# Rotary embedding of an attention head moved from the iteration that uses it to the iteration that projects it, and the attention steps placed from slot 3 instead of slot 6.5

## The chip, the cores and the metric

The kernel runs on one core of a Trainium2 chip. The metric is device time in microseconds, the median of three runs. Five engines work from instruction queues of their own, each strictly in program order: PE (TensorE, matmuls), DVE (VectorE), ACT (ScalarE), POOL (GpSimd) and SP (issues the DMAs). An engine waits for another only where its next instruction carries a wait on a semaphore. A waiting instruction holds back everything behind it on that engine.

## The reference, cut to what matters

A layer with two groups of heads. 16 learned tokens are put ahead of 512 tokens of width 2048, the rows are normed, and one projection gives the columns of both groups. The change touches the second group, eight heads of differential attention. For each head (q and k 128 wide, two maps of 64; v 128 wide):

```
q = apply_rope(q, cos, sin);  k = apply_rope(k, cos, sin)     # x*cos + swap_halves(x)*sin
sc = q_c k_c^T / 8, causal mask, p_c = softmax(sc)            # c = 0, 1; queries in blocks of 128
o = (p_0 - lam * p_1) @ v
o = rms_norm(o, subln_w) * (1 - lambda_init) * silu(g)
```

The mixed heads go through an output projection (2048 by 2048), a norm and a residual add.

## The kernel before, in words

Sizes: D = 2048 features in KT = 16 slices of P = 128, SEQ = 512, META = 16, L = 528 tokens. Every projection is done in three matmuls on split weights (`w_hi`, `w_lo`) and split activations (`hn_hi`, `hn_lo`).

The work runs in 17 iterations i = 0 to 16 (`iterations`, lines 402 to 415). An iteration projects the four column tiles of one head pair or head (q = 0 to 3 in `tile_dve`: in an attention iteration these are `xk` = q, `xv` = k, `xr` = v, and the gate), and at the same time works on the head that the iteration before it projected. Iterations 8 to 15 project the attention heads, 9 to 16 attend (head n = i - 8). 10 to 15 are one loop body. 9 also finishes the other group (`gn` is true there and has placements of its own). 16 projects nothing: its PE stream is the first quarter of the output projection (`out_feature`).

The four tiles are 16 units of four weight slices each, 64 **slots** in an iteration. A slot is one feature slice: three matmuls of 512 columns, or six of 264 for k and v. The order on every engine is written out by generators. Each step of a head's work yields a place, a number in slots, and `upto` issues it when the stream comes to that place. On PE a step at place p stands behind slot p rounded up. DVE sorts its steps, the copies of the tiles among them, by their places (15.6, 31.6 and 47.6 for the copies, 63.6 for the gate). ACT and POOL issue one unit of weights at a time (`split_hi`, `split_lo` for unit k + 3) and behind it all steps with places up to 4k + 3. The split of k waits until PE is through unit k - 1 of this iteration (slot 4k - 1).

The steps of a query block qi = 0 to 3 lie at `attn_at(gn, qi)` plus an offset: +0 scores of both maps (PE, L752, or L749 and L750 for qi = 3), +1 and +2 mask, maximum and its negative (DVE, L1392 to L1394), +3 and +4 exponentials (ACT, L1027), +5 reciprocal and combination (DVE, L1398 to L1401), +7 transposes of the combined map (PE, L757, L759), +8 copy of these (ACT, L1032), +10 the product with v (PE, L765, L767), +11 its copy (DVE, L1405), +11.5 its squares (ACT, L1036). After qi = 3: +12.5 the variance (DVE, L1409), +12.7 the power -1/2 (POOL, L1101), +13 scaling (DVE, L1413), +14 transposes (PE, L773), +14.5 gate and store into the mixed rows (DVE, L1417).

The rotary embedding takes two parts. ACT swaps the halves of 64 (`swap_halves`, L880: four copies of 32 partitions) at places 16.3 (`xk` into `q_swap`) and 32.3 (`xv` into `k_swap`) of the projecting iteration, behind the tile's copy on DVE. DVE then makes seven instructions, L1372 to L1376 for q (into `qpad`) and L1379 to L1382 for k (into `kr`). Before the change these stand at places -0.5 to 0.2 of the next iteration.

Of the kernel before, what the change touches and what calls it, by code (L numbers as in the profile page):

```python
# [30 lines left out]
ALU = mybir.AluOpType  # L31
# [3 lines left out]
P = 128  # L35
D = 2048
SEQ = 512
META = 16
L = SEQ + META
KT = D // P  # L40
RW = 1024
NP_ = RW // P
HD = 64
# [74 lines left out]
def hybrid_layer(nc, x, meta_tokens, pre_norm_w, w_in, rwkv_mu, rwkv_w0, rwkv_w_up, rwkv_a0, rwkv_a_up,  # L118
# [3 lines left out]
    with ctx:  # L122
        def sb(name, shape, dt=F32):
            return ctx.enter_context(nc.sbuf_tensor(name, shape, dt))

        def sem(name):
            return ctx.enter_context(nc.semaphore(name))
# [21 lines left out]
        xk = sb("xk", [P, TP])  # L149
        xv = sb("xv", [P, TP])  # L150
# [86 lines left out]
        cos_t = carve("attn", "cos_t", L)  # L237
        sin_t = carve("attn", "sin_t", L)
        qpad = [carve("attn", f"qpad{m}", SEQ) for m in range(2)]
        kr = carve("attn", "kr", L)  # L240
        vt = carve("attn", "vt", TG * P)
        rt1 = carve("attn", "rt1", L)
        q_swap = carve("attn", "q_swap", SEQ)
        k_swap = carve("attn", "k_swap", L)
# [38 lines left out]
        def s(name):  # L283
            if name not in S:
                S[name] = sem(name)
            return S[name]
# [50 lines left out]
        def attn_stage_at(gn):  # L337
            return 12 if gn else 0

        def attn_at(gn, qi):  # L340
            return 20.5 + 12.2 * qi if gn else 6.5 + 13.0 * qi

        def mixed(i):

# [796 lines left out]
        def _(dve):  # L1141
            V = nc.vector
            steps = Steps(dve, "dve_step")
            TT, STT, TS = V.tensor_tensor, V.scalar_tensor_tensor, V.tensor_scalar
# [52 lines left out]
            def tile_dve(i, proj, work, gn):  # L1197
                for q in range(3):

                    yield 20 if q == 0 and gn and work == "attn" else 16 * q + 15.6  # L1200
                    o = tiles[(q + 1) % 2]
                    xt = (xk, xv, xr)[q]
                    if proj == "rwkv":
                        dve.wait_ge(s("x_based"), i * 3 + (q + 1))
                        STT(xt[:, PAD + 1:TP], o[:, EDGE:EDGE + L - 1], column(par, (8, 16, 0)[q], i),
                            xt[:, PAD + 1:TP], ALU.mult, ALU.add).then_inc(s("tile_freed"), 1)
                    else:
                        dve.wait_ge(s("unit_used"), i * 16 + (8 + 4 * q))
                        if work == "rwkv":
                            dve.wait_ge(s("bonus_taken" if q == 1 else "pads_made"), NP_)  # L1210
                            dve.wait_ge(s("vpad_made"), 2 * NP_)
                        else:
                            if q < 2:
                                dve.wait_ge(s("roped"), (i - NP_) * 2 + (q - 1))
                            else:
                                dve.wait_ge(s("vt_turned"), i - NP_)
                        full = FULL[proj][q]
                        n, at = (L, EDGE) if full else (SEQ, 0)
                        V.tensor_copy(xt[:, 0:n], o[:, at:at + n]).then_inc(s("tile_freed"), 1)
                yield 63.6  # L1220
                dve.wait_ge(s("gate_tanh"), i + 1)
                STT(gate[:], tanh_g[:], 1.0, tiles[0][:, 0:SEQ], ALU.add, ALU.mult).then_inc(s("tile_freed"), 1)
# [118 lines left out]
            def chain_dve(i, g, late, work, gn):  # L1341
                for c in range(GC):
# [10 lines left out]
                    dve.wait_ge(s("s_scaled"), m)  # L1353
                    STT(state, mb[:, 0:P], w_end[:, ch:ch + 1], state0, ALU.mult, ALU.add).then_inc(s("s_taken"), 1)  # L1354

            def attn_dve(i, gn):
                n = i - NP_
                at = attn_stage_at(gn)
                yield 9.3 if gn else at - 0.5
                if gn:  # L1360

                    dve.wait_ge(s("s_taken"), NP_ * NC)
                    dve.wait_ge(s("y_taken"), NP_ * NG)
                    V.memset(qpad[0][HD:P, :], 0.0)
                    V.memset(qpad[1][0:HD, :], 0.0).then_inc(s("arena_freed"), 1)
                yield 15 if gn else at - 0.3
                if gn:
                    dve.wait_ge(s("rope_in"), 32)
                if not gn:
                    dve.wait_ge(s("roped"), n * 2 - 2)  # L1370
                dve.wait_ge(s("tile_freed"), i * 4 - 1)
                steps.quiet(TT(rt1[:, 0:SEQ], xk[:, 0:SEQ], cos_t[:, META:L], ALU.mult))  # L1372
                dve.wait_ge(s("swapped"), n * 8 - 4)
                steps(TT(q_swap, q_swap, sin_t[:, META:L], ALU.mult))
                TT(qpad[0][0:HD, :], rt1[0:HD, 0:SEQ], q_swap[0:HD, :], ALU.add)
                TT(qpad[1][HD:P, :], rt1[HD:P, 0:SEQ], q_swap[HD:P, :], ALU.add).then_inc(s("roped"), 1)  # L1376
                yield 19.2 if gn else at + 0.2
                dve.wait_ge(s("roped"), n * 2 - 1)
                steps.quiet(TT(rt1, xv[:, 0:L], cos_t, ALU.mult))  # L1379
                dve.wait_ge(s("swapped"), n * 8)  # L1380
                steps(TT(k_swap, k_swap, sin_t, ALU.mult))
                TT(kr, rt1, k_swap, ALU.add).then_inc(s("roped"), 1)  # L1382
                for qi in range(4):
                    base = attn_at(gn, qi)
                    c = n * 4 + (qi - 3)
                    at = EDGE if qi == 3 else 0
                    width = META + (qi + 1) * P
                    for m, o in ((0, ma), (1, mb)):
                        yield base + 1 + m
                        dve.wait_ge(s("score_done"), c * 2 + (m - 1))  # L1390
                        d = o[:, at + width - P:at + width]
                        steps(TT(d, d, c32v("causal"), ALU.add))  # L1392
                        steps(V.reduce_max(at_max[:, m:m + 1], o[:, at:at + width], AX))
                        TS(at_neg[:, m:m + 1], at_max[:, m:m + 1], -HD ** -0.5, None,  # L1394
                           ALU.mult).then_inc(s("neg_made"), 1)
                    yield base + 5
                    dve.wait_ge(s("exp_made"), c * 2)
                    steps(V.reciprocal(at_inv, at_sum))  # L1398
                    steps(TT(at_inv[:, 1:2], at_inv[:, 1:2], lam[:], ALU.mult))
                    steps(TS(prob[1][:, 0:width], prob[1][:, 0:width], at_inv[:, 1:2], None, ALU.mult))  # L1400
                    STT(prob[0][:, 0:width], prob[0][:, 0:width], at_inv[:, 0:1], prob[1][:, 0:width], ALU.mult,  # L1401
                        ALU.subtract).then_inc(s("combined"), 1)
                    yield base + 11
                    dve.wait_ge(s("pv_done"), c)
                    V.tensor_copy(o_sb[:, qi * P:(qi + 1) * P], mb[:, 0:P]).then_inc(s("o_taken"), 1)  # L1405
                at = attn_at(gn, 3)
                yield at + 12.5
                dve.wait_ge(s("o_squared"), n * 4)
                TS(at_var, at_var, 1.0 / P, SUB_EPS, ALU.mult, ALU.add).then_inc(s("ovar_taken"), 1)  # L1409
                yield at + 13  # L1410
                dve.wait_ge(s("o_powed"), n)
                o3 = o_sb.rearrange("p (m d) -> p m d", m=4)
                TT(o3, o3, at_pow.unsqueeze(2).broadcast_to([P, 4, P]), ALU.mult).then_inc(s("o_scaled"), 1)  # L1413
                yield at + 14.5
                dve.wait_ge(s("o_turned"), n)
                dve.wait_ge(s("gate_moved"), i)
                STT(mixed(i - 1), gate2[:], gate_sub[:], ma[:, 0:SEQ], ALU.mult, ALU.mult).then_inc(s("o_made"), 1)  # L1417

            def split_y_dve():
                for k in range(KT):  # L1420
                    yield max(4 * k - 7, -1) + 0.1 if k < KT - 1 else 200
                    dve.wait_ge(s("y_hi"), k + 1)
                    TT(hn_lo[:, k, 0:SEQ], ymix[:, k, :], hn_hi[:, k, 0:SEQ].bitcast(F32),  # L1423
                       ALU.subtract).then_inc(s("y_lo"), 1)

            def body(i, proj, work, gn):
                gens = rwkv_work(i, work, gn, stage_dve, gn_dve, inv_dve, chain_dve)
                if work == "attn":
                    gens.append(attn_dve(i, gn))
                gens.append(tile_dve(i, proj, work, gn) if proj is not None else split_y_dve())  # L1430
                upto(begin(*gens), 1000)
                steps.clear()
# [42 lines left out]
```

## Time and profile before

| | us |
|---|---|
| median of three runs (lowest, highest) | 1552.87 (1552.44, 1555.18) |
| span of the profiled execution | 1549.4 |
| PE busy | 1436.7 |
| DVE busy | 767.5 |
| ACT busy | 576.3 |
| POOL busy | 476.7 |
| PE waiting for the rotary embedding (L752 for L1382), 890 to 1410 | 15.3 in 5 waits |

The profile shows one execution. Its own time is the span; the 3.5 us by which the median is longer lie around it (start and end of the program). The iterations with attention begin at about 892 us. The page's chain of the work that ended last is 76% PE. In the lists a row names the line of the code, the engine, the instruction, what it writes and what it reads; what stands in brackets at the end of a timeline row is the idle time before it and what ended it.

### The profile page before, as it was taken

How to read it: one execution, taken by the hardware profiler on the slowest of the kernel's cores; microseconds unless marked ns; L12 is line 12 of the kernel's file. 1: busy time of each engine (PE TensorE's matmuls, PEld its weight loads, DVE VectorE, ACT ScalarE, POOL GpSimd, SP SyncE). 2: the span in 40 equal slices, each digit the busy share in tenths (PEclk: the TensorE clock that was granted, in tenths of full speed). 3: DMA queues.
4: the chain of work that ended last, by engine and by line, in shares of the span. 5: the costliest groups of instructions: out<-in, count | busy, mean ns of one | idle time of the engine just before them, and what ended most of it. 6: DMA issues, size and time to landing. Idle time of an engine off the chain costs nothing.

```text
span 1549.4 us, 26552 instructions
## 1 busy us (share of the span) xinstructions
PE 1436.7 (93%) x9929; PEld 1257.3 (81%) x9929; DVE 767.5 (50%) x1560; ACT 576.3 (37%) x1204; POOL 476.7 (31%) x361
## 2 busy tenths in 40 slices
PE   5998999999999999999999988999999999989994
PEld 4988889788897888988879786978878879768883
DVE  2326566665666666667666544344343443540003
ACT  5332343333434334343333253434444434432321
POOL 2341232222322223232232232334333333324442
PEclk9999999999999999999999999999999999999997
DMA  5221111111111111111111121222222222215322
GB/s 190 71 84 42 42 44 49 50 41 41 42 47 44 43 44 42 47 42 41 47 42 49 50 73 50 70 69 70 69 68 68 61 68 68 68 58 205 117 95 111
DMA packets 151637, 101.43 MB, mean 65 GB/s; under 512 B 6446, under 2 KB 140688, under 8 KB 150416
## 3 DMA queue, kind: packets, MB, share of 16 engines
q1 hardware_dynamic: 151584, 100.71, 21.2%
q8 instruction: 35, 0.57, 0.1%
q14 instruction: 18, 0.15, 0.0%
HBM read 96.49 MB, written 4.19 MB: 65 GB/s over the span
## 4 chain that ended last, share of the span: by engine, by line
PE 76%; DVE 14%; issue 4%; ACT 3%; DMA 1%; POOL 1%; DVEq 0%; SPq 0%; ACTq 0%; POOLq 0%
PE tile L517 39%; PE ma L623 3%; PE tile L784 2%; PE tile L785 2%; PE tile L786 2%; PE ma L644 1%; PE ma L658 1%; DVE arena L1333 1%; PE ma L651 1%; PE mb L709 1%; PE ma L661 1%; DVE arena L1308 1%; PE mb L765 1%; PE ma L786 1%; PE ma L784 1%
## 5 line engine op out<-in xcount | busy, mean ns | idle before, releaser
L1086 POOL TENSOR_TENSOR w_lo<-w_raw,w_hi 128x512 fp32r<-128x512 f32 x324 | 429.3, 1326 | 1012.7 <-ACT w_hi L843 1012.6
L517 PE MATMUL tile<-hn_hi,w_hi 128*128 128x264 f32 (+1 forms) x1696 | 455.5, 331 | 0.0
L517 PE MATMUL tile<-hn_hi,w_lo 128*128 128x264 f32 (+1 forms) x1696 | 436.6, 320 | 0.0
L517 PE MATMUL tile<-hn_lo,w_hi 128*128 128x264 f32 (+1 forms) x1696 | 435.7, 320 | 0.0
L843 ACT CAST w_hi<-w_raw 128x512 fp32r<-128x512 f32 x324 | 200.3, 619 | 425.3 <-PE tile L517 315.1
L517 PEld LDWEIGHTS tile<-hn_hi,w_hi 128*128 128x128 f32 x1696 | 280.0, 190 | 25.6 <-issue 7.2
L517 PEld LDWEIGHTS tile<-hn_hi,w_lo 128*128 128x128 f32 x1696 | 277.6, 190 | 13.3
L517 PEld LDWEIGHTS tile<-hn_lo,w_hi 128*128 128x128 f32 x1696 | 277.3, 190 | 11.0 <-issue 0.5
L1321 DVE TENSOR_TENSOR arena<-ma,c 128x384 f16<-128x384 f32 x120 | 66.7, 556 | 54.7 <-PE ma L644 52.5
L979 ACT ACTIVATE arena<-ma 128x384 f16<-128x384 f32 x120 | 58.5, 487 | 89.0 <-PE ma L658 88.5
L1330 DVE CAST arena<-ma 128x384 f16<-128x384 f32 x120 | 66.6, 555 | 49.3 <-PE ma L661 47.9
L623 PE MATMUL ma<-arena 128*128 128x192 f32 x288 | 59.6, 343 | 12.2 <-issue 12.2
L1405 DVE COPY arena<-mb 128x128 f32<-128x128 f32 x32 | 9.3, 290 | 103.6 <-PE mb L767 103.6
L976 ACT ACTIVATE arena<-ma 128x384 f32<-128x384 f32 x72 | 35.2, 489 | 68.2 <-PE ma L651 68.2
L623 PEld LDWEIGHTS ma<-arena 128*128 128x128 f32 x288 | 47.8, 195 | 15.3 <-issue 13.9
L784 PE MATMUL tile<-w_hi,hn_hi 128*128 128x512 f32 x128 | 53.6, 419 | 5.5 <-DVE hn_lo L1423 5.5
L1308 DVE TENSOR_TENSOR arena<-arena,c 128x384 f16<-128x384 f16 x144 | 52.2, 404 | 0.8
L785 PE MATMUL tile<-w_lo,hn_hi 128*128 128x512 f32 x128 | 51.6, 403 | 0.0
L786 PE MATMUL tile<-w_hi,hn_lo 128*128 128x512 f32 x128 | 51.3, 401 | 0.0
L1101 POOL TENSOR_TENSOR arena<-arena,power 128x4 f32<-128x4 f32 (+2 forms) x25 | 39.1, 1566 | 33.1 <-DVE arena L1409 13.3
L992 ACT ACTIVATE arena<-arena 128x128 f32<-128x128 f32 x72 | 28.8, 400 | 52.7 <-DVE arena L1354 36.5
L658 PE MATMUL ma<-arena 128*128 128x128 f16 x360 | 41.3, 223 | 3.8 <-DVE arena L1321 3.8
(252 smaller groups left out, 2242.5 us busy)
## 6 DMA issues: line engine op xcount, KB each, us to landing
w_raw<-w_in SPq DMA_DIRECT2D x260, 256.0 KB, 2.8
w_raw<-w_out SPq DMA_DIRECT2D x64, 256.0 KB, 2.5
big<-x SPq DMA_DIRECT2D x4, 1024.0 KB, 8.9
arena<-x SPq DMA_DIRECT2D x4, 1024.0 KB, 9.7
out<-big SPq DMA_DIRECT2D x4, 768.0 KB, 3.6
arena<-post_norm_w SPq DMA_DIRECT2D x1, 1024.0 KB, 4.9
out<-big SPq DMA_DIRECT2D x4, 256.0 KB, 2.5
arena<-table_rope SPq DMA_DIRECT2D x2, 264.0 KB, 2.9
```

Of the source, the lines that this page charges most:

```text
L517: last = mm(o[:, at:at + n], w[:, slot, cols], t[:, kt, tok:tok + n], start=(kt == 0 and w is w_hi and t is hn_hi), stop=(kt == KT - 1 and ...
L623: last = mm(ma[:, c * 256:c * 256 + P + CH], pad[:, cs[c], :], apad_r[:, cs[c], :], start=True, stop=True)
L658: last = mm(bank(0, c), bl(xt16, c), bl(z16, c), start=True, stop=True)
L784: mm(banks[t], hn_hi[:, k, y], w_hi[:, k % RING, :], start=(k == 0), stop=False)
L785: mm(banks[t], hn_hi[:, k, y], w_lo[:, k % RING, :], start=False, stop=False)
L786: last = mm(banks[t], hn_lo[:, k, y], w_hi[:, k % RING, :], start=False, stop=(k == KT - 1))
L843: nc.scalar.copy(w_hi[:, slot, :], w_raw[:, slot, :]).then_inc(s("hi_done"), 1)
L979: A(x16, ma[:, 0:W], ACT.Copy).then_inc(s("x_taken"), 1)
L1086: T(w_lo[:, slot, :], w_raw[:, slot, :], w_hi[:, slot, :].bitcast(F32), ALU.subtract).then_inc(s("lo_done"), 1)
L1308: level = lambda l, o: TT(o, g3(ab_hi), level_masks[:, l, :].unsqueeze(1).broadcast_to([P, GC, P]), ALU.mult)
L1321: TT(g3(z16), g3(ma[:, 512:512 + W]), ident16.unsqueeze(1).broadcast_to([P, GC, P]), ALU.add).then_inc(s("zz_taken"), 1)
L1330: V.tensor_copy(xt16, ma[:, 512:512 + W]).then_inc(s("xt_taken"), 1)
```

## The change

- `attn_at` for the iterations without `gn` (10 to 16) gives 3.0 + 13.2 qi instead of 6.5 + 13.0 qi. The four blocks begin at 3, 16.2, 29.4 and 42.6 instead of 6.5, 19.5, 32.5 and 45.5. All steps of the head move with them, on all engines.
- The seven DVE instructions of the rotary embedding become `rope_q` and `rope_k`. A new generator `rope_next`, in every attention iteration that also projects (9 to 15), issues them for the head that is being projected: places 48.2 and 54.5 (62.5 and 64.0 in iteration 9). It first waits until all eight scores of the present head are done, since `qpad` and `kr` have one buffer. Iteration 9 still makes its own head's embedding at 15 and 19.2.
- `swap_halves`, the splits of the weights, the copies of the tiles and the POOL steps keep their code.

```diff
         def attn_at(gn, qi):
-            return 20.5 + 12.2 * qi if gn else 6.5 + 13.0 * qi
+            return 20.5 + 12.2 * qi if gn else 3.0 + 13.2 * qi
...
-            def attn_dve(i, gn):
-                n = i - NP_
-                at = attn_stage_at(gn)
-                yield 9.3 if gn else at - 0.5
...
-                yield 15 if gn else at - 0.3
...
-                if not gn:
-                    dve.wait_ge(s("roped"), n * 2 - 2)
-                dve.wait_ge(s("tile_freed"), i * 4 - 1)
+            def rope_q(n):
+
+                dve.wait_ge(s("tile_freed"), (n + NP_ - 1) * 4 + 2)
                 steps.quiet(TT(rt1[:, 0:SEQ], xk[:, 0:SEQ], cos_t[:, META:L], ALU.mult))
                 dve.wait_ge(s("swapped"), n * 8 - 4)
                 steps(TT(q_swap, q_swap, sin_t[:, META:L], ALU.mult))
                 TT(qpad[0][0:HD, :], rt1[0:HD, 0:SEQ], q_swap[0:HD, :], ALU.add)
                 TT(qpad[1][HD:P, :], rt1[HD:P, 0:SEQ], q_swap[HD:P, :], ALU.add).then_inc(s("roped"), 1)
-                yield 19.2 if gn else at + 0.2
+
+            def rope_k(n):
                 dve.wait_ge(s("roped"), n * 2 - 1)
+                dve.wait_ge(s("tile_freed"), (n + NP_ - 1) * 4 + 3)
                 steps.quiet(TT(rt1, xv[:, 0:L], cos_t, ALU.mult))
                 dve.wait_ge(s("swapped"), n * 8)
                 steps(TT(k_swap, k_swap, sin_t, ALU.mult))
                 TT(kr, rt1, k_swap, ALU.add).then_inc(s("roped"), 1)
+
+            def rope_next(i, gn):
+
+                yield 62.5 if gn else 48.2
+                dve.wait_ge(s("score_done"), (i - NP_) * 8)
+                rope_q(i - (NP_ - 1))
+                yield 64.0 if gn else 54.5
+                rope_k(i - (NP_ - 1))
...
                 if work == "attn":
                     gens.append(attn_dve(i, gn))
+                    if proj is not None:
+                        gens.append(rope_next(i, gn))
```

The order on the engines moves at three places of the loop body (iterations 10 to 15). The first is DVE around the copy of the k tile (`COPY xv`), with the masks and maxima of the third query block (`ma` and `mb` are the scores of the two maps). Before:

```order
L1405 COPY arena<-mb 128x128
L1208 REGISTER_ALU
L1219 COPY xv<-tile 128x528
L1390 ISA
L1392 TENSOR_TENSOR ma<-ma,c 128x128
L1393 TENSOR_REDUCE arena<-ma 128x1
L1394 TENSOR_SCALAR arena<-arena 128x1
L1392 TENSOR_TENSOR mb<-mb,c 128x128
L1393 TENSOR_REDUCE arena<-mb 128x1
L1394 TENSOR_SCALAR arena<-arena 128x1
```

In the changed kernel, where these instructions have line numbers that are 13 higher:

```order
L1418 COPY arena<-mb 128x128
L1403 ISA
L1405 TENSOR_TENSOR ma<-ma,c 128x128
L1406 TENSOR_REDUCE arena<-ma 128x1
L1407 TENSOR_SCALAR arena<-arena 128x1
L1405 TENSOR_TENSOR mb<-mb,c 128x128
L1406 TENSOR_REDUCE arena<-mb 128x1
L1407 TENSOR_SCALAR arena<-arena 128x1
L1208 REGISTER_ALU
L1219 COPY xv<-tile 128x528
L1411 RECIPROCAL arena<-arena 128x2
```

The copy of the k tile stood ahead of the maxima and now stands behind them, ahead of the reciprocal.

The second is ACT in the same stretch: the swap of `xv` and the two exponentials of the third query block (the rows with 128x400).

```order
 L1036 ACTIVATE arena<-arena 128x128
 L842 REGISTER_ALU
 L843 CAST w_hi<-w_raw 128x512
 L880 ACTIVATE arena<-xv 32x528 x4
-L840 ISA
-L842 REGISTER_ALU
-L843 CAST w_hi<-w_raw 128x512
 L1026 ISA
 L1027 ACTIVATE arena<-ma,arena 128x400
 L1027 ACTIVATE arena<-mb,arena 128x400
+L840 ISA
 L842 REGISTER_ALU
```

One split of weights moves from between swap and exponentials to behind them; the swap stays ahead of the exponentials.

The third is DVE at the end of the head. Before, from the copy of the last product with v on:

```order
L1405 COPY arena<-mb 128x128
L1409 TENSOR_SCALAR arena<-arena 128x4
L1413 TENSOR_TENSOR arena<-arena 128x512
L1417 ISA
L1417 SCALAR_TENSOR_TENSOR big<-gate,gate_sub,ma 128x512
```

In the changed kernel:

```order
L1362 TENSOR_TENSOR arena<-arena 64x512
L1363 TENSOR_TENSOR arena<-arena 64x512
L1418 COPY arena<-mb 128x128
L1366 ISA
L1367 REGISTER_ALU
L1368 TENSOR_TENSOR arena<-xv,arena 128x528
L1370 TENSOR_TENSOR arena<-arena 128x528
L1371 TENSOR_TENSOR arena<-arena 128x528
L1422 TENSOR_SCALAR arena<-arena 128x4
L1426 TENSOR_TENSOR arena<-arena 128x512
L1430 ISA
L1430 SCALAR_TENSOR_TENSOR big<-gate,gate_sub,ma 128x512
```

The q part of the embedding (L1359 to L1363) now ends right ahead of the copy, and the k part (L1368 to L1371) stands between the copy and the variance.

## Rows read from the trace of the kernel before

**Rows 1.** The page's first line: the span.

```profile
span 1549.4 us, 26552 instructions
```

**Rows 2.** Waits of PE, 890 to 1410: total us, times, longest.

```profile
PE ma L752 <- DVE arena L1382: 15.3, 5, 3.1
...
PE ma L757 <- DVE arena L1401: 6.1, 5, 2.0
...
PE ma L773 <- DVE arena L1413: 4.4, 2, 3.9
```

**Rows 3.** Waits of PE in the last iteration, 1325 to 1400.

```profile
PE tile L784 <- DVE hn_lo L1423: 5.5, 2, 3.2
...
PE ma L757 <- DVE arena L1401: 3.5, 3, 2.0
```

**Rows 4.** Timeline of DVE, rotary in iteration 12: start us, us.

```profile
1078.12 0.69 DVE L1372 TENSOR_TENSOR arena<-xk,arena 128x512 f32<-128x512 f32 x1
...
1084.34 1.65 DVE L1382 TENSOR_TENSOR arena<-arena 128x528 f32<-128x528 f32 x1
```

**Rows 5.** Timeline of PE, iteration 12: scores, transposes. Start, us, [idle before].

```profile
1086.04 0.51 PE L752 MATMUL ma<-arena 128*128 128x144 f32 x2 [3.05 <-DVE arena L1382]
...
1109.02 0.83 PE L752 MATMUL ma<-arena 128*128 128x400 f32 x2
...
1115.46 0.49 PE L757 MATMUL ma<-c,arena 128*128 128x128 f32 x3
```

**Rows 6.** Timeline of DVE, third query block of iteration 12.

```profile
1107.77 0.71 DVE L1219 COPY xv<-tile 128x528 f32<-128x528 f32 x1 [0.64 <-PE tile L517]
...
1111.83 0.15 DVE L1394 TENSOR_SCALAR arena<-arena 128x1 f32<-128x1 f32 x1
...
1113.83 0.17 DVE L1398 RECIPROCAL arena<-arena 128x2 f32<-128x2 f32 x1 [1.84 <-ACT arena L1027]
...
1114.69 0.64 DVE L1401 SCALAR_TENSOR_TENSOR arena<-arena 128x400 f32<-128x400 f32 x1
```

**Rows 7.** Timeline of ACT, same stretch: swap of xv, first exponential.

```profile
1108.51 2.64 ACT L880 ACTIVATE arena<-xv 32x528 f32<-32x528 f32 x4
...
1112.54 0.59 ACT L1027 ACTIVATE arena<-ma,arena 128x400 f32<-128x400 f32 x1
```

**Rows 8.** Timeline of POOL, iteration 16.

```profile
1365.61 1.38 POOL L1086 TENSOR_TENSOR w_lo<-w_raw,w_hi 128x512 fp32r<-128x512 f32 x1 [1.51 <-ACT w_hi L843]
```

**Rows 9.** Timeline of DVE, iteration 16, beside that POOL instruction.

```profile
1365.91 1.52 DVE L1401 SCALAR_TENSOR_TENSOR arena<-arena 128x400 f32<-128x400 f32 x1
```

**Rows 10.** Timeline of PE, end of the head of iteration 12.

```profile
1130.93 1.05 PE L765 MATMUL mb<-arena 128*128 128x128 f32 x8
...
1133.82 0.39 PE L517 MATMUL tile<-hn_hi,w_hi 128*128 128x512 f32 x1
...
1135.22 0.65 PE L773 MATMUL ma<-c,arena 128*128 128x128 f32 x4
```

**Rows 11.** Timeline of ACT, same stretch: a weight split.

```profile
1130.42 0.62 ACT L843 CAST w_hi<-w_raw 128x512 fp32r<-128x512 f32 x1 [0.66 <-PE tile L517]
```

**Rows 12.** Timeline of POOL, same stretch: that unit's low part, the power.

```profile
1131.12 1.26 POOL L1086 TENSOR_TENSOR w_lo<-w_raw,w_hi 128x512 fp32r<-128x512 f32 x1 [1.95 <-ACT w_hi L843]
...
1133.43 1.01 POOL L1101 TENSOR_TENSOR arena<-arena,power 128x4 f32<-128x4 f32 x1 [1.05 <-DVE arena L1409]
```

**Rows 13.** Timeline of DVE, end of iteration 9.

```profile
949.80 0.29 DVE L1405 COPY arena<-mb 128x128 f32<-128x128 f32 x1 [2.67 <-PE mb L767]
```

**Rows 14.** Windows of 8 us after long PE waits: busy; then clock, DMA, GB/s.

```profile
1023.40:1031.40 8.00, 7.96 (x32) 6.60 (x33) 2.42 (x10) 1.99 (x7) 1.28 (x1) 0.81 0.11 33
...
1086.00:1094.00 8.00, 7.96 (x44) 6.85 (x44) 3.11 (x11) 3.19 (x9) 2.00 (x2) 1.00 0.22 64
...
1208.30:1216.30 8.00, 7.99 (x24) 6.52 (x25) 2.42 (x10) 1.56 (x5) 0.98 (x1) 0.63 0.11 33
...
953.60:961.60 8.00, 7.95 (x30) 6.53 (x31) 5.36 (x8) 1.88 (x4) 1.08 (x1) 0.71 0.13 36
```

More of the change, by code:

```diff
@@ L1354, in chain_dve @@
                     STT(state, mb[:, 0:P], w_end[:, ch:ch + 1], state0, ALU.mult, ALU.add).then_inc(s("s_taken"), 1)
-            def attn_dve(i, gn):
-                n = i - NP_
-                at = attn_stage_at(gn)
-                yield 9.3 if gn else at - 0.5
[L1360 to L1365, printed above, removed]
-                yield 15 if gn else at - 0.3
-                if gn:
-                    dve.wait_ge(s("rope_in"), 32)
-                if not gn:
-                    dve.wait_ge(s("roped"), n * 2 - 2)
-                dve.wait_ge(s("tile_freed"), i * 4 - 1)
+            def rope_q(n):
+                dve.wait_ge(s("tile_freed"), (n + NP_ - 1) * 4 + 2)
                 steps.quiet(TT(rt1[:, 0:SEQ], xk[:, 0:SEQ], cos_t[:, META:L], ALU.mult))
@@ L1382, in attn_dve @@
                 TT(kr, rt1, k_swap, ALU.add).then_inc(s("roped"), 1)
+            def rope_next(i, gn):
[4 more added lines that the diff above has]
+                rope_k(i - (NP_ - 1))
+            def attn_dve(i, gn):
+                n = i - NP_
+                if gn:
+                    yield 9.3
+                    dve.wait_ge(s("s_taken"), NP_ * NC)
+                    dve.wait_ge(s("y_taken"), NP_ * NG)
+                    V.memset(qpad[0][HD:P, :], 0.0)
+                    V.memset(qpad[1][0:HD, :], 0.0).then_inc(s("arena_freed"), 1)
+                if gn:
+                    yield 15
+                    dve.wait_ge(s("rope_in"), 32)
+                    rope_q(i - NP_)
+                    yield 19.2
+                    rope_k(i - NP_)
                 for qi in range(4):
```

## The prediction, made before the changed kernel was run

> **What bounds the kernel now.** I read the page first, for its span of 1549.4 us [rows 1]. The median of the three runs is 3.5 us above it; I work out a change of the span and add it to the median. PE carries the chain that ended last, so what counts is where PE waits. In the list of PE's waits for the attention stretch the largest entry is the first scores of a head waiting for the last instruction of the rotary embedding, 15.3 us in 5 waits, the longest 3.1 [rows 2]. These are iterations 11 to 15. The other two entries are small and partly in iterations 9 and 16: transposes waiting for the combined map, and the last transposes waiting for the scaling. In a loop iteration PE waits for nothing else of size. Next come the timelines of one steady iteration, 12, engine by engine, to find how much room each chain has before its PE step. A slot takes 0.70 us (three matmuls of 512) or 0.73 (six of 264): two slots and the product with v take 2.89 and four slots with it 4.29 in rows 10, so a slot there is 0.70.
>
> **What goes.** The seven embedding instructions run from 1078.12 to 1085.99 and the scores start 0.05 later, after 3.05 us of idle PE [rows 4, 5]. Moved into the iteration before, they have ended about 15 slots before the scores need them. The scores at slot 3 then wait for the copy of v only, which ACT makes at the start of the iteration within two slots. So 15.3 us go. Iteration 10 has no such wait, and the first of the seven attending iterations has its own embedding as before, so there is nothing more to win here. After the five waits TensorE's granted clock is 1.00 over 8 us in two iterations (one shown), 0.81 and nearly that in two (one shown), 0.63 in one [rows 14]: in three of five cases the clock fell to its lower level (1.2 of 2.4 GHz) after the wait. That costs 8 x (0.19 + 0.19 + 0.37) = 6.0 us, 1.2 a wait. It goes as well, if nothing takes its place.
>
> **What comes: the swap ahead of the third block's exponentials.** Let S be the start of that block's scores on PE. In iteration 12 S is 1109.02 and the transposes start at S + 6.44, seven slots after the scores, without a wait [rows 5]. The second maximum is ready at 1111.83 + 0.15, S + 2.96 [rows 6]. Before the change ACT had finished the swap of `xv` by then: it began at 1108.51, right behind the copy of the tile at 1107.77, and took 2.64 us [rows 6, 7]. Now the scores stand behind slot 30 and the copy of the k tile belongs behind slot 31. DVE makes the copy behind both maxima: S + 3.0 to S + 3.7. The swap waits for it and stands ahead of the exponentials in ACT's queue: S + 3.7 to S + 6.4. From the first exponential to the reciprocal it is 1.29 us (1112.54 to 1113.83), from the reciprocal to the end of the combination 1.50 (1113.83 to 1114.69 + 0.64) [rows 6, 7]. That gives S + 9.2 against the 6.44 of PE's stream: a wait of at least 2.8 us in each of the six loop iterations.
>
> It is likely more. The next split on ACT (0.62 us, rows 11) is overdue and follows the exponentials at S + 7.7, and POOL makes its low part 0.7 later, as 1130.42 to 1131.12 shows [rows 11, 12]: from S + 8.4 to S + 9.7. The last instruction of the combination would start at S + 8.5. In iteration 16 the same instruction started 0.30 us behind such a POOL instruction and took 1.52 instead of 0.64 us, until after that one's end [rows 6, 8, 9]. The same here ends it at S + 10.3, a wait of 3.9. I take 3.9; the ends are 2.8 and 4.1. The Trainium skill says the same of the mechanism (SBUF — State Buffer, "Who interferes with whom"): a DVE instruction with two SBUF inputs contends with a GpSimd instruction that reads SBUF, and whoever issues first blocks the other. The trace agrees; by the rule the value is 3.9, and without it 2.8.
>
> **What comes: the end of the head.** Let V be the start of the last product with v, 1130.93 in iteration 12 [rows 10]. The last transposes were at V + 4.29, four slots on, just in time: the power on POOL began at 1133.43, 1.79 before them [rows 10, 12]. POOL makes it behind the low part of unit 17, for which ACT's split waits for the end of slot 55. Before, V lay behind slot 56, so that low part started at 1131.12, V + 0.2, which is 0.9 after slot 55's end (slot 56 of 0.70 lies between). Now V lies behind slot 53, slot 55 ends at V + 2.9, the low part runs from V + 3.8 to V + 5.1, the power cannot start earlier, and the transposes are at V + 6.9 instead of V + 4.29, a wait of 2.6 us. The place of the power, 55.3 instead of 58.2, falls into the same unit on POOL, so its order does not change; only PE arrives three slots earlier.
>
> DVE adds to it. The k part of the embedding, three instructions of 0.7 without a collision [rows 4], stands between the copy and the variance: copy at V + 1.6, variance at V + 4.0 instead of just ahead of the power, V + 2.3. That alone is inside the 5.1 of POOL. But its last instruction runs when the low part wants to start, which pushes that by some 0.3. If the q part, which runs beside two low parts, collides twice (1.0 each, as 1.65 against 0.69 in rows 4), the copy comes late, the k part collides too, and the wait is 3.9. I take 2.9; the ends are 2.6 and 3.9.
>
> **Iterations 9 and 16.** In 9 the seven instructions, 7 x 0.7 = 4.9 us, now stand ahead of the last product's copy, before which DVE was idle for 2.67 [rows 13]. The copy comes 2.2 later, and PE's wait for the scaling grows from 3.9 [rows 2] to 6.1: +2.2. In 16 the embedding leaves the start, where no PE wait hung on it. Its 3.5 us of waits for the combined map [rows 3] come from exponentials held behind a split, and at the new places they stand ahead of it: I take 2.5 less, the end being about even, since the late power costs PE there too while the last feature needs less of a wait. Bounds: 3.5 less to 2 more.
>
> **The clock.** A wait of 3.88 us in iteration 9 is followed by 8 us at 0.71 [rows 2, 14], 2.3 us lost. Six new waits of 3.9 at 2.3 and six of 2.9 at 1.2 make 21, less the 6.0 that go: +15. The ends: none of the twelve lowers the clock, -6, and all do at 3.0 (8 x 0.37), +30. This is the widest term.
>
> **The sum.** -15.3 + 6 x 3.9 + 6 x 2.9 + 2.2 - 2.5 = +25.2 us of waiting, +15 of clock: +40. The span comes to 1590 and the median to 1593. The cheaper ends of the waits (2.8, 2.6) with a clock term of 0 give 1552.9 + 16.8, about 1570. The dearer ones (4.0 and 3.4) with +25 give 1552.9 + 28.8 + 25, about 1607.
>
> **The rivals.**
> - Only the swap costs. The power might be issued so that PE does not miss it, for which nothing speaks but that the old order had no wait there. -15.3 + 23.4 + 2.2 - 2.5 = +7.8, clock 13.8 - 6 = +8: 1569. Chance 0.07.
> - Only the end of the head costs, because ACT would be done with the swap earlier than I think (the copy of the k tile is free from slot 31's end on). -15.3 + 17.4 - 0.3 = +1.8, clock +1: 1556. Chance 0.04.
> - Faster: neither chain is late, since the waits of one shift the slots under the other and DVE, at half load, catches up. It decides only if the swap ends about 3 us earlier, which needs the copy of the k tile at S, before PE has run the slot that completes the tile. Then -15.3 - 6 - 2.5 = -24: 1529. Chance 0.03.
> - The change doesn't do what it says: the embedding is late in its new place too, held by the wait for all scores. That wait is met by slot 43, five slots ahead. The time would be near 1556 or above with the new waits still there. Chance 0.01.
> - The forecast, both new waits in each loop iteration: 0.85.
>
> **How the numbers follow.** The predicted time is the forecast's 1593. The range 1568 to 1608 takes in the bounds of both waits and most of the clock's, and the rival at 1569. About 0.2 of the chance lies outside, most of it in the clock and in iterations where only one wait is full. A change of 0.2%, 3.1 us, is about what a measurement of this kernel can tell from none. Faster 0.03, within 0.03, slower 0.94.
>
> **What would show it.** Right: PE's waits for the embedding are gone; six new waits of the third block's transposes for the combination, 2.8 to 4 us, with the swap of `xv` ended just before the first exponential of that block on ACT; six waits of the last transposes for the scaling of 2.6 to 3.9, with a low part on POOL ending where the power starts; more stretches at the lower clock. Wrong: exponentials of the third block that start within a microsecond of the maximum, or a power that starts within 3 us of the product with v.

## The result, and the profile after

The changed kernel takes 1588.05 us (median of 4 runs, 1587.03 to 1590.11) against 1553.02 of the kernel before on the same chip: 1.0225 times as long, interval 1.0211 to 1.0240. The forecast was 1593 us in a range of 1568 to 1608. The profiled execution took 1587.26 us, its span is 1585.5 us, 36.1 more than before. In every execution the time is 1.8 us above the span, so of the 3.5 us that the prediction put between span and median only 1.8 lie around the program; the rest is spread between executions.

Where the time went stands in the list of PE's waits. This is the changed kernel, 880 to 1440 us (total, times, longest); its lines L1414, L1426 and L1436 are L1401, L1413 and L1423 of before.

```profile
PE ma L757 <- DVE arena L1414: 23.8, 8, 3.5
PE ma L773 <- DVE arena L1426: 23.0, 8, 5.9
PE tile L784 <- DVE hn_lo L1436: 5.9, 2, 3.2
```

The 15.3 us of the first scores waiting for the rotary embedding [rows 2] are gone. The transposes of a combined map wait 23.8 us instead of 6.1, the last transposes 23.0 instead of 4.4. Set against the same list of before over the same stretch, where L784 has 5.5, these waits grow by 21.4 us in sum (52.7 against 31.3). The other 14.7 of the 36.1 are not waits.

As in the prediction, S is the start of the third block's scores on PE (here 1118.30) and V that of the last product with v (1146.78). One loop iteration on PE, 12, answers to [rows 5, 10]: first scores, third block's scores and transposes, last product with v, last transposes.

```profile
1095.14 0.41 PE L752 MATMUL ma<-arena 128*128 128x144 f32 x2
...
1118.30 0.83 PE L752 MATMUL ma<-arena 128*128 128x400 f32 x2
...
1128.41 0.90 PE L757 MATMUL ma<-c,arena 128*128 128x128 f32 x3 [3.50 <-DVE arena L1414]
...
1146.78 1.05 PE L765 MATMUL mb<-arena 128*128 128x128 f32 x8
...
1153.63 0.66 PE L773 MATMUL ma<-c,arena 128*128 128x128 f32 x4 [2.38 <-DVE arena L1426]
```

The first scores have no wait in brackets: the embedding had ended 12.5 us before them (1150.67, and 1163.20 for the next head's scores), somewhat more than the 15 slots, 10.5 us, of the prediction. The third block's transposes start at S + 10.11 instead of S + 6.44, the last ones at V + 6.85 instead of V + 4.29. The idle in brackets is some 0.2 less than the growth of these distances (3.67 and 2.56), since it counts from the modelled end of the last matmul.

Behind the first of the two waits stands ACT. Its timeline in the same iteration, answering to [rows 7]:

```profile
1122.02 2.65 ACT L880 ACTIVATE arena<-xv 32x528 f32<-32x528 f32 x4 [0.83 <-DVE xv L1219]
1124.69 0.59 ACT L1027 ACTIVATE arena<-ma,arena 128x400 f32<-128x400 f32 x1
...
1125.85 0.61 ACT L843 CAST w_hi<-w_raw 128x512 fp32r<-128x512 f32 x1
```

The swap waits for the copy of the k tile on DVE, then holds the first exponential until S + 6.39; the maxima had been ready since S + 2.96. DVE there, answering to [rows 6]:

```profile
1121.11 0.15 DVE L1407 TENSOR_SCALAR arena<-arena 128x1 f32<-128x1 f32 x1
1121.28 0.71 DVE L1219 COPY xv<-tile 128x528 f32<-128x528 f32 x1
1125.99 0.17 DVE L1411 RECIPROCAL arena<-arena 128x2 f32<-128x2 f32 x1 [4.00 <-ACT arena L1027]
...
1126.85 1.51 DVE L1414 SCALAR_TENSOR_TENSOR arena<-arena 128x400 f32<-128x400 f32 x1
```

L1414 took 1.51 us instead of 0.64. POOL's low part began 0.31 us ahead of it and it ends 0.43 after that one, the same pattern as [rows 8, 9]. POOL in this iteration, the low part beside L1414 and the two instructions at the end of the head, answering to [rows 12]:

```profile
1126.54 1.39 POOL L1086 TENSOR_TENSOR w_lo<-w_raw,w_hi 128x512 fp32r<-128x512 f32 x1 [3.98 <-ACT w_hi L843]
...
1150.57 1.31 POOL L1086 TENSOR_TENSOR w_lo<-w_raw,w_hi 128x512 fp32r<-128x512 f32 x1 [3.02 <-ACT w_hi L843]
1151.84 1.00 POOL L1101 TENSOR_TENSOR arena<-arena,power 128x4 f32<-128x4 f32 x1
```

The low part of unit 17 begins at V + 3.8 and the power follows it without a gap, at V + 5.06. DVE had the variance ready before that in this iteration:

```profile
1150.59 0.16 DVE L1422 TENSOR_SCALAR arena<-arena 128x4 f32<-128x4 f32 x1
1152.88 0.69 DVE L1426 TENSOR_TENSOR arena<-arena 128x512 f32<-128x512 f32 x1 [2.13 <-POOL arena L1101]
```

Iteration 12 is one of two in which it is so (10 is the other). In the other four the variance starts just behind the start of the low part and takes 1.28 us instead of 0.16; the power starts 0.1 us later for it, and PE waits 2.50 us instead of 2.38. Iteration 11, where that low part starts at 1082.39 and the power at 1083.77:

```profile
1082.41 1.28 DVE L1422 TENSOR_SCALAR arena<-arena 128x4 f32<-128x4 f32 x1
```

Iteration 16 has no embedding at the end of its head, and V is 1414.25 there. Its power starts at V + 5.08 all the same, and its last transposes wait 2.40 us:

```profile
1419.33 1.01 POOL L1101 TENSOR_TENSOR arena<-arena,power 128x4 f32<-128x4 f32 x1
```

The granted clock of TensorE, in windows of 8 us after the two waits (it is the number ahead of the last two), answering to [rows 14], and over 400 us of the loop, where it was 0.98 before:

```profile
1128.40:1136.40 8.00, 7.99 (x41) 7.64 (x42) 0.29 (x1) 1.66 (x5) 1.27 (x1) 0.62 0.21 60
1153.60:1161.60 8.00, 7.97 (x33) 6.50 (x34) 1.43 (x2) 2.09 (x4) 1.57 (x2) 0.79 0.19 56
960.00:1360.00 400.00, 364.26 (x2138) 320.33 (x2137) 153.24 (x347) 149.81 (x356) 130.25 (x101) 0.94 0.21 62
```

After each of the twelve new waits of iterations 10 to 15 the clock falls to its lower level: their windows show 0.62 to 0.82.

### The profile page after: what moved, and what is told of

Its sections match the earlier page's. It is cut to its first block, busy times and chain, and to the rows that moved or that the text cites. A ratio compares the mean times of both kernels' runs of the same rounds, so it can differ in the third digit from the quotient of the medians.

```text
span 1585.5 us, 26560 instructions
## 1 busy us (share of the span) xinstructions
PE 1452.5 (92%) x9929; PEld 1272.7 (80%) x9929; DVE 766.9 (48%) x1560; ACT 577.4 (36%) x1204; POOL 473.4 (30%) x361
## 4 chain that ended last, share of the span: by engine, by line
PE 57%; issue 21%; DVE 10%; POOL 8%; ACT 2%; DMA 1%; POOLq 0%; DVEq 0%; SPq 0%; ACTq 0%
PE tile L517 24%; POOL w_lo L1086 8%; PE ma L623 3%; PE tile L784 2%; PE tile L786 2%; PE tile L785 2%; PE ma L644 1%; PE ma L658 1%; DVE arena L1333 1%; PE ma L651 1%; PE mb L709 1%; PE ma L661 1%; DVE arena L1308 1%; PE ma L786 1%; PE ma L784 1%
## 5 line engine op out<-in xcount | busy, mean ns | idle before, releaser
L517 PE MATMUL tile<-hn_hi,w_hi 128*128 128x264 f32 (+1 forms) x1696 | 461.5, 335 | 0.0
L517 PE MATMUL tile<-hn_hi,w_lo 128*128 128x264 f32 (+1 forms) x1696 | 441.6, 324 | 0.0
L517 PE MATMUL tile<-hn_lo,w_hi 128*128 128x264 f32 (+1 forms) x1696 | 440.9, 323 | 0.0
L517 PEld LDWEIGHTS tile<-hn_hi,w_hi 128*128 128x128 f32 x1696 | 284.5, 193 | 25.8 <-issue 7.2
L517 PEld LDWEIGHTS tile<-hn_hi,w_lo 128*128 128x128 f32 x1696 | 282.1, 193 | 13.8
L517 PEld LDWEIGHTS tile<-hn_lo,w_hi 128*128 128x128 f32 x1696 | 282.4, 193 | 11.1 <-issue 0.5
L623 PEld LDWEIGHTS ma<-arena 128*128 128x128 f32 x288 | 47.0, 193 | 15.2 <-issue 13.9
L784 PE MATMUL tile<-w_hi,hn_hi 128*128 128x512 f32 x128 | 53.5, 418 | 5.9 <-DVE hn_lo L1436 5.9
```

What stands on the lines that cost most here:

```text
L517: last = mm(o[:, at:at + n], w[:, slot, cols], t[:, kt, tok:tok + n], start=(kt == 0 and w is w_hi and t is hn_hi), stop=(kt == KT - 1 and ...
L623: last = mm(ma[:, c * 256:c * 256 + P + CH], pad[:, cs[c], :], apad_r[:, cs[c], :], start=True, stop=True)
L784: mm(banks[t], hn_hi[:, k, y], w_hi[:, k % RING, :], start=(k == 0), stop=False)
```

## The experiments

Each kernel was timed beside the kernel before on the same chip; ratios are to that one. The experiments ran on three chips, on which the kernel before took 1552.62 to 1553.44 us, so that differences between two experiments of under some 2 us say little.

**e1: the swap behind the exponentials.**

```diff
-                        yield 20.8 if gn and f == 0 else 16 * f + 16.3
+                        yield 20.8 if gn and f == 0 else (16.3, 34.5)[f]
```

> The changed kernel with the swap of the k tile on ACT issued at place 34.5 instead of 32.3, behind the two exponentials of the third query block. Theory (the swap holds the exponentials): the six waits of 3.5 us before the third block's transposes go, 21 us, and with them about half of what the lower clock costs, some 8; the six waits of 2.4 at the last transposes stay. Time near 1559. Rival (the room between the third block's scores and its transposes is too small whatever stands on ACT): the waits stay at 2.5 to 3.5 and the time above 1580.

1553.15 us, ratio 1.0002 (0.9990 to 1.0015). One number of the ACT order takes back the whole loss. PE's waits, 880 to 1440:

```profile
PE ma L773 <- DVE arena L1426: 23.0, 8, 5.9
PE tile L784 <- DVE hn_lo L1436: 5.9, 2, 3.2
PE ma L757 <- DVE arena L1414: 2.8, 2, 1.7
```

The waits of 3.5 us went in all six iterations, 21.0 us; the last transposes still wait as much as before. The room between scores and transposes was enough. The time fell by 34.9 us, 13.9 more than these waits, and ended 6 us below what was expected. The list of iteration 16 did not change and the six waits of 2.4 us still stand, so what is left for this excess is the clock after the longer waits: their six windows in the changed kernel miss 12.4 us of full clock together. The expectation had put 8 there.

**e2: the k part of the embedding behind the store.**

```diff
-                yield 64.0 if gn else 54.5
+                yield 64.0 if gn else 58.0
```

> The changed kernel with the k part of the rotary embedding on DVE at place 58.0 instead of 54.5, behind the head's last store instead of ahead of the variance. Theory (the power on POOL waits for the low part of unit 17, which ends at the product with v + 5.1): the variance comes 1.7 us earlier, the last transposes still wait 2.4 us in each loop iteration, and the time stays within 3 us of 1588. Rival (the embedding ahead of the variance makes the wait): the wait falls to 0.7 and the time by 10 us or more.

1585.41 us, 2.6 less, with a ratio of 1.0209 (1.0189 to 1.0229) that is hardly apart from the 1.0225 of the changed kernel. The variance came 1.7 us earlier, and PE did not profit: L773 has 22.4 us in its list instead of 23.0. First DVE, then PE:

```profile
1148.94 0.17 DVE L1422 TENSOR_SCALAR arena<-arena 128x4 f32<-128x4 f32 x1 [0.47 <-ACT arena L1036]
1152.75 0.69 DVE L1426 TENSOR_TENSOR arena<-arena 128x512 f32<-128x512 f32 x1 [3.63 <-POOL arena L1101]
```

```profile
1153.50 1.11 PE L773 MATMUL ma<-c,arena 128*128 128x128 f32 x4 [2.35 <-DVE arena L1426]
```

So the moved embedding was not the cause of this wait, as long as the power stands behind the low part.

**e3: the power ahead of the low part.**

```diff
-                yield attn_at(gn, 3) + 12.7
+                yield attn_at(gn, 3) + 12.3
```

> The changed kernel with the power on POOL issued 12.3 instead of 12.7 slots after the fourth block's start, which puts it ahead of the low part of unit 17 in POOL's queue; the embedding stays ahead of the variance. Theory: the power now starts with the variance, at the product with v + 4.0 instead of + 5.1, so the wait at the last transposes falls from 2.4 to 1.2 us, 7 us over six iterations, with 2 to 6 us of clock: 1575 to 1580. Rival (DVE's embedding alone sets it): no change.

1581.40 us, 6.6 less, a time just above what was expected, but not by the way expected. The power started at V + 4.0 as foreseen (1149.45), yet the wait at the last transposes stayed at 2.43 us in the loop:

```profile
1149.45 1.01 POOL L1101 TENSOR_TENSOR arena<-arena,power 128x4 f32<-128x4 f32 x1 [3.27 <-DVE arena L1422]
1150.42 1.26 POOL L1086 TENSOR_TENSOR w_lo<-w_raw,w_hi 128x512 fp32r<-128x512 f32 x1
```

```profile
1150.49 1.75 DVE L1426 TENSOR_TENSOR arena<-arena 128x512 f32<-128x512 f32 x1 [1.12 <-POOL arena L1101]
```

The low part, now behind the power in POOL's queue, starts 0.07 us ahead of the scaling, which then takes 1.75 instead of 0.69, in all six loop iterations alike. The collision ate the gain. What was won is iteration 16's wait of 2.4 (the list of L773 has 20.4 us in 7 waits instead of 23.0 in 8). The rest goes with the clock, which fell after only four of the six waits of 2.43 us: two of the windows behind them show 1.00.

**e9: both.** The edits of e2 and e3 together.

> The changed kernel with both moves at the end of the head: the k part of the embedding at 58.0 and the power at +12.3; the swap stays ahead of the exponentials. After the k part alone (wait 2.35 us, 3 us faster) and the power alone (wait 2.43 us, 7 us faster), the theory is that two causes stand behind one another: with the power behind the low part the end of that sets the time, and with the k part ahead of the variance the scaling meets the low part. Both moved: the variance at the product with v + 2.3, the power at once, the scaling ended or begun before the low part; the six waits at the last transposes go (under 0.3 us each), those of 3.5 stay, and the time is near 1565. Rival (the q part makes the copy of the product late): a wait of 1 us or more is left.

1561.52 us, 26.5 less than the changed kernel and 3.5 below the expectation. The list has one wait of L773 left, that of iteration 9; L757 keeps its 3.5 six times:

```profile
PE ma L757 <- DVE arena L1414: 25.3, 9, 3.5
...
PE ma L773 <- DVE arena L1426: 5.9, 1, 5.9
```

The two causes stand one behind the other: alone each move gives 2.6 or 6.6 us and leaves the wait in the loop, together they take it away and give 26.5.

**e4 and e5: the two parts of the change apart.** e4 is the kernel before with the first line of the change; e5 the changed kernel without it.

```diff
-            return 20.5 + 12.2 * qi if gn else 6.5 + 13.0 * qi
+            return 20.5 + 12.2 * qi if gn else 3.0 + 13.2 * qi
```

> The kernel before with the new places alone (3.0 + 13.2 qi); the rotary embedding stays at the start of the iteration that uses it. Theory (both new waits come from the places, not from the moved embedding): the third block's transposes wait 3.5 us and the last ones 2.4 in each loop iteration as in the changed kernel, and the first scores, four slots earlier, wait 3.05 + 4 x 0.7 = 5.9 us for the embedding. Against the kernel before that is 5 x 2.8 + 2 + 6 x 5.9 - 2 = +49 us, and some 20 for the clock: near 1620. Rival (the moved embedding makes the new waits on DVE): they are under 1 us here, and the time is near 1575.

1626.15 us (expected near 1620), ratio 1.0475 (1.0459 to 1.0491). PE's waits, 880 to 1460:

```profile
PE ma L752 <- DVE arena L1382: 27.6, 7, 4.9
PE ma L757 <- DVE arena L1401: 25.3, 9, 3.5
PE ma L773 <- DVE arena L1413: 20.4, 8, 3.9
```

Both new waits are there, 3.5 and 2.35 us in the loop, without any embedding at the end of the head. They belong to the places. The first scores wait 4.9 us and not the 5.9 expected: the last instruction of the embedding took 0.71 us here and 1.65 before [rows 4].

> The changed kernel with the old places (6.5 + 13.0 qi); the embedding of the next head stays at 48.2 and 54.5. Theory: the wait of 3.05 us at the first scores goes, the third block's transposes and the last transposes wait for nothing, but the q part of the embedding now stands ahead of the fourth block's combination on DVE, whose transposes wait 2.5 to 3.5 us. Sum: -15.3 + 6 x 3 + 2 (iteration 9) and some 3 of clock: near 1561. Rival (the moved embedding is as costly as the whole change): above 1580 with waits of the last transposes.

1560.81 us, ratio 1.0051 (1.0036 to 1.0067), as expected. The q part ahead of the fourth block's reciprocal makes one wait of 3.19 us a loop iteration:

```profile
1133.92 1.12 PE L757 MATMUL ma<-c,arena 128*128 128x128 f32 x4 [3.19 <-DVE arena L1414]
```

**e6: the waits filled with matmuls.** Their results are read by nobody.

```diff
                     yield base + 7
+                    if qi == 2 and not gn:
+                        for _ in range(14):
+                            mm(mb[:, 512:1024], hn_hi[:, 0, 0:P], hn_hi[:, 0, 0:SEQ], start=True, stop=True)
...
                 yield at + 14
+                if not gn:
+                    for _ in range(10):
+                        mm(mb[:, 512:1024], hn_hi[:, 0, 0:P], hn_hi[:, 0, 0:SEQ], start=True, stop=True)
```

> The changed kernel with matmuls whose result nobody reads put into the two waits of each iteration without the other group's norm: 14 of 128x512 ahead of the third block's transposes, 10 ahead of the last ones (3.2 and 2.3 us of TensorE work). It computes the same output. Theory (some 15 us of the 35 are the lower clock that follows the waits): the granted clock stays at its upper level in iterations 10 to 16, the waits shrink to what the fillers leave, and the time falls to about 1573. Rival (the clock costs nothing, the slow matmuls only fill what would be waited for later): the time stays at 1588 or rises.

1572.64 us, 15.4 less than the changed kernel, with 168 matmuls of 128x512 more (24 in each of iterations 10 to 16). The mean clock over 960 to 1360 is 0.99 instead of 0.94, and 0.3 and 0.2 us are left of the two waits:

```profile
960.00:1360.00 400.00, 393.64 (x2348) 341.89 (x2348) 163.54 (x363) 159.44 (x378) 134.82 (x105) 0.99 0.22 64
```

The order of the work is as in the changed kernel and only the idle time is filled, so this measures the clock's term by itself. It is best read over the loop alone. The first scores of iteration 10 and of iteration 16 start at 961.52 and 1368.20 us in the changed kernel, at 964.00 and 1352.40 in e6: 406.7 and 388.4 us, 18.3 less. The whole time fell by less since the filler in the third block of iteration 16 fills no wait (it is 3.4 us of PE in the loop) and the stretch ahead of iteration 10 was 2.5 us longer in this execution. So twelve waits of 3.5 and 2.4 us cost 18.3 us on top of their idle time, 1.5 each.

**e7 and e8: versions that keep the gain.** e7 is the changed kernel with the three moves (34.5, 58.0, +12.3), and the k part at 72.0 in iteration 9. e8 keeps the old places, and puts only the embedding elsewhere:

```diff
-            return 20.5 + 12.2 * qi if gn else 3.0 + 13.2 * qi
+            return 20.5 + 12.2 * qi if gn else 6.5 + 13.0 * qi
...
-                yield 62.5 if gn else 48.2
+                yield 62.5 if gn else 51.2
...
-                yield 64.0 if gn else 54.5
+                yield 72.0 if gn else 61.0
```

> The changed kernel with the swap of the k tile at 34.5, the k part of the embedding at 58.0 (72.0, behind the store, in iteration 9) and the power at +12.3. Theory: all three causes are gone, PE waits in iterations 10 to 15 for next to nothing, iteration 9 is back at 3.9 us, and against the kernel before the 15.3 us of waits and 6 of clock are won: near 1530. Rival (something else is late at these places, such as the copy of the product behind the q part): waits of 1 us and more at the last transposes remain, above 1540.

> The changed kernel with the old places (6.5 + 13.0 qi) and the embedding of the next head behind the fourth block's combination (q part, 51.2) and behind the store (k part, 61.0; 62.5 and 72.0 in iteration 9). Theory: the first scores' wait goes and nothing takes its place, so the time is 1553 - 15.3 - 6, near 1532, without any change on ACT and POOL. Rival (the start of the head must move to gain): at least 1545.

e7 (expected near 1530): 1524.60 us, ratio 0.9822 (0.9809 to 0.9836), the fastest here. e8 (expected near 1532): 1529.89 us, ratio 0.9859 (0.9844 to 0.9874). In e7 PE is busy for all of 960 to 1300, at full clock:

```profile
960.00:1300.00 340.00, 340.00 (x2130) 300.89 (x2129) 148.98 (x347) 148.63 (x355) 131.34 (x101) 1.00 0.25 73
```

Against the kernel before e8 wins 23 us with 15.3 us of waits removed. The rotary move as such was worth 1.4%. What makes e7 5 us faster than e8 was not looked into.

**e10: iteration 9 alone.** The changed kernel with `yield 72.0 if gn else 54.5` for the k part.

> The changed kernel with the k part of the embedding behind the store in iteration 9 (72.0 instead of 64.0), all else unchanged. Theory: PE's wait for the scaling in iteration 9 falls from 5.86 to 3.9 us, and the first scores of iteration 10 still find the embedding ready: 2 us faster, up to 4 with the clock, 1584 to 1586. Rival: the wait moves to the first scores of iteration 10 and the time stays at 1588.

1586.75 us against 1588.05, measured on different chips; 1.3 us is not clear of the spread. The trace shows the wait itself: 3.88 us instead of 5.86, and the first scores of iteration 10 still without one.

```profile
953.48 1.12 PE L773 MATMUL ma<-c,arena 128*128 128x128 f32 x4 [3.88 <-DVE arena L1426]
...
959.41 0.41 PE L752 MATMUL ma<-arena 128*128 128x144 f32 x2
```

## Why the prediction was right

| step, us | forecast | measured |
|---|---|---|
| first scores' waits | -15.3 | -15.3 |
| third block, six waits | 6 x 3.9 | 6 x 3.5 |
| last transposes, six waits | 6 x 2.9 | 6 x 2.4 |
| iteration 9, L773 | +2.2 | +2.0 (3.88 to 5.86) |
| iteration 16 | -2.5 | +0.5 |
| clock, net | +15 | +14.7, what is left of the span's 36.1 and not measured by itself |

The measured rows, without the clock's, add up to some 1.5 us more than the 21.4 of the lists; the last paragraph of this section says where these went.

- **What goes** is shown by e5 and e8 together: neither has a wait at the first scores, and in e8, with the embedding moved and nothing late behind it, the kernel is 23 us faster.
- **The swap** is shown by e1. The chain in the trace fits step by step: second maximum at S + 2.96 as read from before, swap ended at S + 6.37, reciprocal at S + 7.69 (forecast 7.7), combination ended at S + 10.06 (forecast 10.3). The collision was real, and a little cheaper since the low part began 0.2 earlier.
- **The end of the head** had its bound right: power at V + 5.06 (forecast 5.1), transposes at V + 6.85 (forecast 6.9). The embedding did not push the low part, which began at V + 3.8 as without it; the 0.3 that I added for this came as 0.1 by another way, through the variance, in four of six iterations. The dear end of 3.9 did not come either, since the copy of the product was not late. e2 and the head of iteration 16 show that DVE's part was behind cover, e9 that both causes have to go. That moving the power alone would halve the wait, expected of e3, was wrong: it met a collision that the trace before had shown once, in iteration 9 (the scaling took 1.74 us there, 0.06 behind the start of a low part), and that I did not carry over.
- **Iteration 16** is the step with the wrong sign. Its waits for the combined map fell from 3.5 to 1.7 us, not to 1.0: the third and the fourth block's went, but the second block's combination now took 1.54 us beside a low part and PE waited 1.71 for it. The last transposes rose from 0.5 to 2.4; the wait of L784 rose from 5.5 to 5.9. I had taken the end as about even, and it cost 2.3. The step is 3 us off in 40.
- **The clock** came out at its forecast size, partly by luck. The twelve windows behind the new waits miss 22.2 us of full clock against 21 in the forecast, but otherwise distributed: 2.1 a wait of 3.5 us instead of 2.3, and 1.6 a wait of 2.4 instead of 1.2, because the level fell after all six of these. In time e6 gives 18.3 us for the twelve; less the 6.0 that go with the old waits this is 12.3 net, a little under the 15. The 2.4 us between that and the 14.7 of the table are not split up.

Against the forecast of +40 the span grew by 36.1: the waits of the loop came 5.4 us below the forecast (6 x 0.9), iteration 9 0.2 below, iteration 16 3 above, the clock 0.3 below, and 1.5 went where the sum had no term (below). In the median another 0.9 is missing, since it lies 2.6 us above the profiled span here and not 3.5. The range's top was worked out with waits of 4.0 and 3.4 us, although the ends named before were 4.1 and 3.9; with those it would be 3.6 us higher, which changes nothing here.

The 1.5 us are the wait of 1.54 for the first block's combination in iteration 9 of before, inside the 6.1 of [rows 2], which is not in the changed kernel. Nothing that the change moves stands there. Over the 8 us from that block's scores the granted clock is 1.00 before and 0.79 in the changed kernel, and the weight split of ACT that waits for PE starts at 911.19 us instead of 909.72. The low part behind it starts at 911.89 instead of 910.42, no longer beside the combination. First before, then the changed kernel:

```profile
910.57 1.28 DVE L1401 SCALAR_TENSOR_TENSOR arena<-arena 128x144 f32<-128x144 f32 x1
```

```profile
910.49 0.37 DVE L1414 SCALAR_TENSOR_TENSOR arena<-arena 128x144 f32<-128x144 f32 x1
```

All twelve traces agree: the wait is there in the seven with the clock at 1.00 in this window (before, e4, e6, e7, e8, e9, e10) and missing in the five with 0.79. So it goes with the clock of the single execution and not with the change. Why the clock fell there in some executions stays open.

## What to carry to other kernels

When a step is moved in a hand-written order, list for every engine what the moved step now stands behind, not only what it stood behind on the engine that waited: here scores issued some three slots earlier on PE met an ACT swap and a POOL low part whose places in their own queues had stayed. A chain that was just in time (here to within 0.1 us of the transposes) has no room to be pulled forward unless its slowest supplier moves too. Price an idle matmul engine at more than its idle time: here twelve waits of 35 us together cost 18 us more by the lower clock after them.

## What the runs showed of the hardware that was not expected

- Waits of 2.4 to 2.5 us were followed by the lower clock level in six of six loop iterations of the changed kernel, of e1, e2 and e4, in five of six of e10 and in four of six of e3, while waits of 3.05 us in the kernel before were so in three of five and those of 3.2 us in e5 in three of six. All waits of 3.5 us were. So the length of the wait alone did not decide it here; what did is not shown.
- Beside POOL's 1.3 us `w_lo` instruction the combination took 1.51 us instead of 0.64 and the scaling 1.75 instead of 0.69. Even the variance, 0.16 us with one SBUF input of 128x4, took 1.28 when it started 0.02 us behind that instruction. An instruction that waits for POOL's result meets POOL's next one: in all six loop iterations of e3, and in iteration 9 of before, the low part started less than 0.1 us ahead of the scaling.
- Two moves worth 2.6 and 6.6 us alone are worth 26.5 together.
